# Gate weights split one stage ahead, branch weights split in the scan, and a scan's first loads on two queues

## What is computed

```python
h = rms_norm(x, pre_norm_w[l])
p = h @ w_cat
p_rwkv, p_conv, p_pool, p_gate = jnp.split(p[..., :N_IN], [...], axis=-1)
...
y_a, v_layer = rwkv7_branch(token_shift(p_rwkv, mu_shift[l]), ...)   # 8 heads of 64, a scan over the tokens
y_b = short_conv_branch(p_conv, conv_w[l])
y_c = pool_branch(p_pool, pool_w[l], pool_scale[l])
...
gates = jax.nn.sigmoid(p_gate.reshape(bsz, slen, N_BRANCH, D_MODEL))
merged = jnp.einsum('bsnd,nbsd->bsd', gates, proj)
x = x + rms_norm(merged @ w_out[l], post_norm_w[l])
```

## Time and profile before

| | us |
|---|---|
| median of 3 runs | 2592.15 (2591.79 to 2596.54) |
| the profiled execution | 2588.1 |
| its span, first to last instruction | 2586.0 |
| TensorE busy | 2457.9 (95%) |
| VectorE, ScalarE, GpSimd busy | 1102.2, 773.8, 863.0 |
| scan, first gate matmul to last matmul | 240.04 to 753.11 |
| first matmul of the branches | 759.09 |

### The profile page before, as it was taken

How to read it: one execution, slowest core, us unless ns; L and a number is a source line. 1 busy time by engine, 2 the same in 40 slices (tenths; PEclk the granted TensorE clock), 3 DMA queues, 4 the chain that set the end, 5 groups by cost and what they waited for, 6 DMA issues and landing times. The chain is left out here.

```text
span 2586.0 us, 43591 instructions
## 1 busy us (share of the span) xinstructions
PE 2457.9 (95%) x18356; PEld 1960.9 (76%) x18356; DVE 1102.2 (43%) x1336; ACT 773.8 (30%) x1213; POOL 863.0 (33%) x517
## 2 busy tenths in 40 slices
PE   5997999999999999999999998989989999999999
PEld 4775777777777888778777876767768888887887
DVE  5444222222212434454364556754378666661000
ACT  3323222222212111143342104542354333332210
POOL 0234222222201222234363431035336545555621
PEclk8998999999999999999999998999999999999999
DMA  6244233333121112144433331022322222224431
GB/s 187 90 152 152 78 88 96 87 86 90 46 87 41 49 58 58 34 148 138 147 96 108 82 101 37 17 74 78 134 76 90 75 86 92 65 97 142 151 114 65
DMA packets 258581, 238.77 MB, mean 92 GB/s; under 512 B 35888, under 2 KB 218416, under 8 KB 258416
## 3 DMA queue, kind: packets, MB, share of 16 engines
q1 hardware_dynamic: 251536, 224.28, 27.7%
q10 hardware_dynamic: 6880, 12.06, 1.7%
HBM read 166.80 MB, written 61.90 MB: 88 GB/s over the span
## 5 line engine op out<-in xcount | busy, mean ns | idle before, releaser
L177 POOL TENSOR_TENSOR wlo<-wraw,whi 128x1024 fp32r<-128x1024 f32 x87 | 216.8, 2492 | 655.9 <-ACT whi L172 644.3
L3182 PE MATMUL tl_ps_bank<-tl_dn,tl_hid 128*128 128x512 f32 x1056 | 241.4, 391 | 2.5 <-POOL tl_dn L2882 2.5
L3182 PEld LDWEIGHTS tl_ps_bank<-tl_dn,tl_hid 128*128 128x128 f32 x1056 | 199.4, 189 | 44.3 <-issue 2.9
L1023 PE MATMUL rs_ps_bank<-hT_hi,rs_f_hi 128*128 128x512 f32 x384 | 172.3, 449 | 25.1 <-POOL rs_f_lo L787 14.8
L172 ACT CAST whi<-wraw 128x1024 fp32r<-128x1024 f32 x87 | 91.2, 1048 | 319.3 <-PE br_ps_ps L199 117.6
L199 PE MATMUL br_ps_ps<-hT_hi,whi 128*128 128x512 f32 x448 | 177.9, 397 | 6.0 <-PEq L107 6.0
L199 PE MATMUL br_ps_ps<-hT_hi,wlo 128*128 128x512 f32 x448 | 176.1, 393 | 0.0
L199 PE MATMUL br_ps_ps<-hT_lo,whi 128*128 128x512 f32 x448 | 175.9, 393 | 0.0
L2720 PE MATMUL tl_ps_bank<-tl_M,tl_ophi 128*128 128x512 f32 x528 | 167.1, 390 | 0.0
L1023 PE MATMUL rs_ps_bank<-hT_lo,rs_f_hi 128*128 128x512 f32 x384 | 153.1, 399 | 0.0
L1023 PE MATMUL rs_ps_bank<-hT_hi,rs_f_lo 128*128 128x512 f32 x384 | 152.7, 398 | 0.0
(11 more groups left out here) (439 smaller groups left out, 5561.6 us busy)
## 6 DMA issues: line engine op xcount, KB each, us to landing
wraw<-in_w_in SPq DMA_DIRECT2D x78, 512.0 KB, 4.3
scratch_pg<-rs_f_out SPq DMA_DIRECT2D x48, 256.0 KB, 2.5
wraw<-in_w_out SPq DMA_DIRECT2D x24, 512.0 KB, 3.7
tl_raw<-in_w_gate SPq DMA_DIRECT2D x11, 1024.0 KB, 6.8
tl_raw<-in_w_up SPq DMA_DIRECT2D x11, 1024.0 KB, 5.4
scratch_hid<-tl_H SPq DMA_DIRECT2D x11, 1024.0 KB, 4.9
tl_hidraw<-scratch_hid SPq DMA_DIRECT2D x22, 512.0 KB, 3.3
tl_dnraw<-in_w_down SPq DMA_DIRECT2D x44, 256.0 KB, 2.7
```

What stands on the lines that cost most here:

```text
L177: self.nc.gpsimd.tensor_tensor(self.lo[s][:, :], self.raw[s][:, :], self.hi[s][:, :].bitcast(F32), ALU.subtract).then_inc(self.lo_ready, 1)
L1023: ins = mm(F[:, h, :], a[:, c], b[:, k, cols[h]], start=k == 0 and u == 0, stop=k == KD - 1 and u == 2)
L3182: ins = nc.tensor.matmul(bank[b][:, :], hid[k][:, x, c], dn[n % 2][:, v, :], start=k == 0 and j == 0, stop=k == FF - 1 and j == 2)
```

## The change

- The projection's `following` weights are now the gate weights (0, 0) and (0, 1), not the branches' first two. Its separate load of (0, 0) and the waits for it are gone.
- In the scan the hi and lo halves for x = 0 and 1 are those of the `Weights` slots, so the first two gate weights are already split when the scan starts. The counters of the two halves start at 3, so that nobody waits for them.
- The branches' first two weights are loaded and split in the scan: at products 21 and 22, Sync loads one after the two stores, ScalarE (`station`) casts it after its copy of the product, and GpSimd (`lows`) makes the low half.
- For block 0 ScalarE issues the four loads of the runs and the three of v, and then the gate weight (0, 2). Sync issues a, r, b and k, then the identity and the two masks.
- VectorE waits for the constants only after the preparation of block 0 and the first output copy, GpSimd only after its part of the preparation.

```diff
@@ phase_rwkv_in
-                w.wait_split(sp, N)
-                sp.dma_start(w.raw[1][:, :].rearrange("p (k c) -> p k c", k=KD), merge_source(d, 0, 0)).then_inc(gate_in, 16)
                 second_stores(3)
                 bonus_store(3)
-                sp.wait_ge(gate_in, 16)
...
@@ phase_rwkv_scan
-        f_raw = [w.raw[1][:, :], w.raw[0][:, :], sh.sb("f_raw", [P, KD * P])[:, :]]
-        f_hi, f_lo = ([sh.sb(f"{n}{x}", [P, KD * P], F32R) for x in range(TILES)] for n in ("f_hi", "f_lo"))
+        w.phase(sh)
+        slots = [w.slot(0), w.slot(1)]
+        f_raw, f_hi, f_lo = ([ring[u][:, :] for u in slots] + [sh.sb(n, [P, KD * P], dt)[:, :]]
+                             for n, ring, dt in (("f_raw", w.raw, F32), ("f_hi", w.hi, F32R), ("f_lo", w.lo, F32R)))
...
+            def load_runs(eng, i):
+                at_run = slice(2 * i * PAD, 2 * (i + 1) * PAD)
+                chunk_run = lambda j: slice((2 * i + j) * PAD, (2 * i + j + 1) * PAD)
+                eng.dma_start(run[:, :, :], d.rl[:, :, at_run]).then_inc(runs, 16)
+                to, of = by_swap(run_sw[:, :, :]), by_swap(d.rl)
+                eng.dma_start(to[:, 0, :, :], of[:, 0, :, at_run]).then_inc(runs, 16)
+                for r in range(2):
+                    eng.dma_start(to[:, 1, :, r * PAD:(r + 1) * PAD], of[:, 1, :, chunk_run(1 - r)]).then_inc(runs, 16)
+
+            def load_swapped(eng, i, n, src):
+                to, of = by_swap(raw[n][:, :, :]), by_swap(src)
+                eng.dma_start(to[:, 0, :, :], of[:, 0, :, i * P:i * P + P]).then_inc(loaded, 16)
+                for r in range(2):
+                    eng.dma_start(to[:, 1, :, half[r]], of[:, 1, :, i * P + (1 - r) * C:i * P + (2 - r) * C]).then_inc(loaded, 16)
...
@@ Sync
-                sp.dma_start(eye[:, :], d.const("eye")).then_inc(consts, 16)
...
+                def load_block(i, runs_too=True):
+                    at = slice(i * P, i * P + P)
+                    if runs_too:
+                        load_runs(sp, i)
                     for n, src in (("a", d.ra), ("r", d.rr)):
                         sp.dma_start(raw[n][:, :, :], src[:, :, at]).then_inc(loaded, 16)
                     for n, src in (("b", d.rb), ("k", d.rk), ("v", d.rv)):
+                        if n != "v" or runs_too:
+                            load_swapped(sp, i, n, src)
...
                         next_weights(t + 4)
+                        if t in (N - 3, N - 2):
+                            w.load(sp, t - N + 5, t - N + 3, following[t - N + 3])
...
-                load_block(0)
+                load_block(0, False)
+                sp.dma_start(eye[:, :], d.const("eye")).then_inc(consts, 16)
                 sp.dma_start(gmask[:, :], d.const("gmask")).then_inc(consts, 16)
...
@@ GpSimd
+                pool.sem_inc(f_lo_ready.sem, 3)
...
                     for t in ended(i, first, last):
+                        if t in (N - 3, N - 2):
+                            w.split_lo(pool, t - N + 5, t - N + 3)
                         if t + 3 < N:
                             low(pool, (t + 3) // TILES, t % TILES)
 
-                low(pool, 0, 0)
-                pool.wait_ge(consts, 48)
                 pool.wait_ge(cleared, 2)
                 prepare(pool, 0)
-                low(pool, 0, 1)
+                pool.wait_ge(consts, 48)
                 fresh()
                 low(pool, 0, 2)
                 low(pool, 1, 0)
...
@@ ScalarE
+                act.sem_inc(f_hi_ready.sem, 3)
...
-                act.sem_inc(f_in[0], 16)
-                gate_weights(act, 0, 1)
-                high(act, 0, 0)
+                for x in range(2):
+                    act.sem_inc(f_in[x], 16)
+                load_runs(act, 0)
+                load_swapped(act, 0, "v", d.rv)
                 gate_weights(act, 0, 2)
                 act.wait_ge(runs, 64)
                 for n in range(3):
                     grow(0, n)
-                high(act, 0, 1)
                 high(act, 0, 2)
 
                 def station(i, first, last):
                     for t in ended(i, first, last):
                         out(t // TILES, t % TILES)
+                        if t in (N - 3, N - 2):
+                            f_product.wait(act, t // TILES, 2 * (t % TILES) + 2)
+                            w.split_hi(act, t - N + 5, t - N + 3, 1)
...
@@ VectorE
-                dve.wait_ge(consts, 48)
...
                 for n in range(3):
                     prepare(0, n)
                 out(0, 0)
+                dve.wait_ge(consts, 48)
...
@@ TensorE
+                pe.sem_inc(w.product, 4)
...
@@ program
-                phase_rwkv_in(nc, d, w, hT, R, two(lambda t: branch_source(d, t)))
-            phase_rwkv_scan(nc, d, w, hT)
+                phase_rwkv_in(nc, d, w, hT, R, two(lambda x: merge_source(d, 0, x)))
+            phase_rwkv_scan(nc, d, w, hT, two(lambda t: branch_source(d, t)))
```

## The result

| | before | after |
|---|---|---|
| median | 2592.4 | 2597.28 (2593.57 to 2599.39) |
| ratio, 95% interval | | 1.0016 [1.0009, 1.0023] |
| the profiled execution, its span | 2588.1, 2586.0 | 2595.07, 2592.6 |

Each has 16 runs. The ratio is + 4.1 us (2.3 to 6.0), and in a second comparison + 4.9 us (1.0019 [1.0010, 1.0028]). The forecast was + 6.3. So the change makes the kernel slower, by a little less than the 0.2% that I had called the least a measurement can tell.

The account below looks back on a forecast made before the run. The prediction took TensorE, busy 95% of the span, to bound the kernel. Start - 4.2, block 7's stalls + 7.5 and clock + 3.0 made + 6.3 us on 2592.15, so 2598.4, range 2592.1 to 2605.0.

Parts of the forecast that it names:

- projection 0: Projection: gate weights replace branch weights with the same bytes, casts and subtractions, so cost 0.
- the moved waits 0: Scan start: VectorE's wait for the masks, moved after the first output copy, costs 0.
- the second queue's bytes: Scan start: the block loads, 1.8 MB at 288 GB/s, need 6.3 us from 234, so the bytes suffice.
- the chain copy, store issue, load, landing, cast, PM copy: Block 7, products 21 and 22: TensorE stalls 4.6 and 2.9 us behind ScalarE's wait for the weight; together 7.5.
- The rival of a real gain: Block 7: ScalarE's wait binds nobody, leaving only the start's gain, - 5.5 us (2586.7); chance 0.06.
- the term of the start: Scan start: first product and block 0's transposes come earlier; gain 4.2 us, taken between 3.7 and 5.5.
- the fast one of my two ends: Scan start: every ScalarE issue takes 0.66 us, preparation ends near 247.6, under the first product; gain 5.5 us.
- the slow end of my forecast: Scan start: ScalarE's first issue takes 3.26 us, preparation ends at 250.1, after the product; gain 3.7 us.
- the clock: 3.0 forecast: Block 7: TensorE's granted clock falls to 0.50 around both stalls, costing 1.5 us each, 3.0 together.
- My price of 1.5 for each gap: Block 7: a 3.30 us low clock loses 0.45 per us, 1.5 per gap; at most 2.4, at least 0.
- The clock holds: Block 7: the stalls are as computed but the clock falls in neither; + 3.3 us, 2595.4; chance 0.17.
- Shared engines: Scan start: gate weights and masks interleave with block loads; gain 2.7, total + 7.8 to + 9.3, 2600.7; chance 0.12.

Follow-up runs that it names:

- e1_early: The change with both branch weights loaded one product earlier (after products 20 and 21); ratio 0.9985 against the kernel before.
- e2_block7: The change with the start of the scan put back as it was before, block 7 as in the change; ratio 1.0045 against the kernel before.
- e6_masks: The change with identity issued first and identity and masks awaited before block 0's preparation, two queues kept; one execution, 2597.9 us (before 2592.8).
- e3_busy: The change with 19 and 11 idle matmuls added in block 7's two stalls, keeping TensorE busy; ratio 1.0022 against the kernel before.
- e4_again: Second run of the change with only the first branch weight loaded one product earlier; ratio 0.9994 against the kernel before.
- e9_early22: The change with only the second branch weight loaded one product earlier; one execution, 2594.4 us (before 2593.1).
- e0: The change itself, unedited, measured again beside the other kernels; ratio 1.0019 against the kernel before.
- e5: The change with all of block 0's loads on Sync's queue, masks still last; one execution, 2598.0 us (before 2588.9).
- e8: The change with block 0's loads all on Sync's queue, identity first and masks awaited before the preparation; one execution, 2600.3 us (before 2588.9).
- e1_again: Second run of the change with both branch weights loaded one product earlier; ratio 0.9975 against the kernel before.

## Why the prediction was right and where it was not

**Right, by its own steps.** The direction and the range; projection 0 (- 0.3); the moved waits 0; the second queue's bytes were no bound. In block 7 the chain copy, store issue, load, landing, cast, PM copy came link by link: stalls of 4.59 and 2.93 against 4.6 and 2.9, the casts waiting for the DMA, ScalarE's in-order queue holding the PM copy. The work moved into block 7, two casts and two low halves, cost nothing (e1_early). The rival of a real gain needed TensorE to be late for another reason; it wasn't.

**Mis-sized, the term of the start: 4.2 forecast, 5.5 to 6.5 measured** (6.5 against before, 5.5 against the old start in e2_block7). TensorE's first product, not the preparation, bounds it, as at the fast one of my two ends, whose gain was 5.5. Three parts of that step:
- The choice between the ends. I took the slow first issue of 3.26 us for a property of the first issue on ScalarE's queue. With a run load in first place it took 0.67. Where a 512 KB gate weight is first, it is slow again (3.06 and 3.25 in the two fences above, 3.31 in e2_block7); as eighth issue it took 0.80 at 237.62. So I had copied a duration over to another kind of transfer. That it is this load in first place, and not the moment, rests on four slow cases and no test by itself.
- The preparation's length. I kept 6.06 us; it took 3.83 (241.93 to 245.76). Two rows of before were longer for what GpSimd did beside them. The product bt took 2.88 beside GpSimd's low half (0, 1), which is gone from there; it took 1.78 here beside GpSimd's product r, and 1.09 in e6_masks, half of it beside GpSimd's copy of the identity. The copy of v took 1.55 before and 0.43 here, with GpSimd's product k beside it both times: only the order of the two starts differs (last section). I had named the cause and then written that the work beside would stay the same. With 3.83, even the slow end of my forecast (241.4 + 2.6 + 3.8 = 247.8) would have lain under the product, which I had ending at 248.2.
- The product took 246.99 - 234.14 = 12.85 and not 13.7: the low clock lasted 3.98 us (9 matmuls) and not 5.25 (12). I had taken this length as fixed, but it isn't the change's: under the old start it is 13.73 (before) and 12.77 (e2_block7), under the unedited new start 12.51 to 13.34. This 0.9 us of the gain was luck.

**Mis-sized, the clock: 3.0 forecast, 3.9 to 4.1 measured.** The mechanism holds: e3_busy takes it away with the length of the stalls kept, and the loss goes. My price of 1.5 for each gap was that of one low stretch of 3.3 us. Here the first lasted some 3.4 us and the second 6.8, of which some 3.3 and 5.9 lay behind the stalls; at my 0.45 for each us that makes 4.1, so in the change the rate was right and the length wrong. My upper bound of 2.4 for one gap was too low as well: e4_again paid 2.6 and e9_early22 2.85. Over the six executions with both stalls (the change, e0, e2, e5, e6, e8) the price runs from 2.9 to 4.1; in the cheapest, e6, both stretches were short. So 3.0 was near the lower edge, not the middle.

**The sum.** - 4.2 + 7.5 + 3.0 = + 6.3 became - 6.5 + 7.5 + 4.0 = + 5.0, less 1.2 of projection and blocks 0 to 6 together, in which I can show no cause. The two errors had opposite signs, so the total was nearer than its parts, which is luck.

**The rivals.** "The clock holds" is wrong for both stalls together, though for a lone stall of 2.9 us it was true once in two executions. "Shared engines" asked for transposes after 250 and a wait; there was none. But what the Trainium skill says in "DMA: Bandwidth & Descriptors", section "Issuing engines are not separate DMA queues", that a second issuing engine saves only the issuing time, usually small beside the transfer, this case bears out with the masks last: going back to one queue cost some 0.6 us (e5_onequeue). I gave that rule the wrong consequence: it doesn't say that the second queue hurts. With the masks awaited first the second queue was worth 26.82 - 24.36 = 2.5 us, so there the issuing time was not small. About half of the start's gain or more doesn't come from the loads' order at all: the weights split ahead give 3.6 alone (30.40 - 26.82; 2.6 against e2_block7's 29.46), since the first product no longer waits for GpSimd; the two load edits together add 2.8, and either one alone 2.2 to 2.5 of it.

**The odds.** I put 0.50 on slower by over 0.2%, which I took for the least that can be told. The measured 0.16% lies under that, and yet its whole interval lies above 1: with 16 runs each the least that can be told was smaller.

## What to carry to other kernels

A step that splits or casts a prefetched tile on an engine with an in-order queue must not come in the same step that issues the load: count when the load lands against what stands in the queue behind the wait, and issue one stage earlier (here 11.6 us for moving two loads). A stall of a busy TensorE of some 3 to 5 us must be priced with the clock behind it, and as a range, as the same stall of 2.9 us cost once nothing and once 2.6 us more. A duration read beside other work, or from a queue's first transfer, belongs to that neighbourhood: before carrying it over, ask which neighbour made it long and whether it will still be there.

## What the runs showed of the hardware that I had not expected

- The granted clock after equal gaps isn't fixed: 2.90 us of waiting kept 1.00, 2.91 us in the same place of the same kernel gave 0.50. (The two executions were on two chips.) Low stretches in block 7 were either some 3.4 or some 6.8 us long, in either order.
- The clock also falls within dense work: in the projection, with TensorE busy throughout (6.00 of 6.00, clock 0.72), in some executions and not in others. The five falls of e1_early, e1_again and e3_busy there, between 132 and 174 us, all came 0.5 to 1.2 us behind a run of 16 short matmuls (128x2, 1.92 us together); the change has the same 16 without a fall.
- A 512 KB gate weight took ScalarE 3.06 to 3.31 us to issue as its first transfer of the execution (before, e2, e5, e8) and 0.80 as its eighth (the change); a load of the runs took 0.67 as the first.
- VectorE's copy of v (128x512) for block 0 took 0.43 us in the ten executions where it began 0.06 to 0.07 us before GpSimd's product and 1.55 to 1.56 in the four where it began 0.01 to 0.02 after it (before, e2_block7, e6_masks, e8_presplit). These four are also the ones that await the masks first, so that the order of the two is the cause was not tried by itself. The rows below are e6_masks, VectorE and GpSimd.

```profile
246.29 1.55 DVE L939 COPY rs_vt<-rs_in_v 128x512 f32<-128x512 f32 x1 [9.02 <-DMA rs_level<-in_consts]
...
249.47 1.09 DVE L945 TENSOR_TENSOR rs_bt<-rs_in_b,rs_g_inv 128x512 f32<-128x512 f32 x1
...
246.27 1.29 POOL L801 TENSOR_TENSOR rs_kt<-rs_in_k,rs_g_inv 128x512 f32<-128x512 f32 x1 [15.51 <-DMA rs_level<-in_consts]
```
